# Row scaling in the sparse-attention and forgetting heads: from GpSimd to VectorE

## What is computed

```
logits = einsum(q, k) * scale + decay          # forgetting heads
p = softmax(where(causal, logits, NEG_INF))
o = p @ v

e = where(mask, exp(z - max(z)), 0)            # sparse attention, three branches
p = e / max(sum(e), 1e-30)
out = gate0 * (p_c @ v_c) + gate1 * (p_s @ v_s) + gate2 * (p_w @ v_w)
```

## Time and profile before

| | us |
|---|---|
| median of 3 runs | 2121.92 (2121.44 to 2124.77) |
| the profiled execution, its own time | 2123.0 |
| span of the profiled execution | 2121.1 |
| PE busy | 2072.8 |
| DVE busy | 1036.2 |
| ACT busy | 810.8 |
| POOL busy | 247.1 |

### The profile page before, as it was taken

The page is one execution under the profiler, slowest core; times in us unless marked ns, Lnnn a source line. Parts: engine busy times, 40 slices in busy tenths (PEclk is TensorE's granted clock), DMA queues, the critical chain, the costliest instruction groups (busy, mean ns, idle before and its releaser), DMA issues.

```text
span 2121.1 us, 25763 instructions
## 1 busy us (share of the span) xinstructions
PE 2072.8 (98%) x10471; PEld 1679.3 (79%) x10471; DVE 1036.2 (49%) x1872; ACT 810.8 (38%) x1543; POOL 247.1 (12%) x276
## 2 busy tenths in 40 slices
PE   7999999999999999999999999999999999999998
PEld 6767788888888767788888888878766788888887
DVE  6464454334436364454334436746556445433443
ACT  4355452222234355452222225344456334222222
POOL 2004410000002004310000002000267000000000
PEclk9999999999999999999999999999999999999999
DMA  5433333233322312233233332422321224323321
GB/s 157 119 65 74 97 103 99 96 95 99 94 90 76 100 50 67 81 97 100 95 94 100 95 95 57 114 62 79 87 60 31 85 90 124 100 90 100 100 95 65
DMA packets 269513, 189.42 MB, mean 89 GB/s; under 512 B 18156, under 2 KB 239524, under 8 KB 269396
## 3 DMA queue, kind: packets, MB, share of 16 engines
q1 hardware_dynamic: 264080, 174.28, 28.1%
q0 software_dynamic: 5168, 13.47, 2.6%
q10 hardware_dynamic: 148, 0.04, 0.0%
HBM read 183.53 MB, written 4.23 MB: 89 GB/s over the span
## 4 chain that ended last, share of the span: by engine, by line
PE 92%; DVE 4%; ACT 2%; POOL 1%; issue 1%; DMA 0%; DVEq 0%; ACTq 0%; POOLq 0%
PE bank L635 53%; PE bank L681 9%; PE bank L683 9%; PE bank L682 9%; PE bank L770 3%; PE bank L737 2%; PE bank L756 2%; PE bank L694 1%; PE bank L865 1%; DVE weights_hi_lo L1035 1%; PE bank L867 1%; PE bank L866 1%; ACT arena L1761 1%; PE bank L742 1%; DVE h_features L1073 1%
## 5 line engine op out<-in xcount | busy, mean ns | idle before, releaser
L635 PE MATMUL bank<-h_features,weights_hi_lo 128*128 128x512 f32 (+1 forms) x5088 | 1115.9, 380 | 5.1 <-DVE weights_hi_lo L1035 4.2
L635 PEld LDWEIGHTS bank<-h_features,weights_hi_lo 128*128 128x128 f32 x5088 | 916.8, 189 | 188.7 <-issue 6.4
L1035 DVE TENSOR_TENSOR weights_hi_lo<-weights,weights_hi_lo 128x1024 fp32r<-128x1024 f32 (+2 forms) x337 | 396.5, 1181 | 491.8 <-ACT weights_hi_lo L1702 491.1
L1702 ACT ACTIVATE weights_hi_lo<-weights 128x1024 fp32r<-128x1024 f32 (+2 forms) x337 | 337.8, 1007 | 276.3 <-PE bank L683 250.8
L681 PE MATMUL bank<-weights_hi_lo,hidden 128*128 128x512 f32 x528 | 205.8, 390 | 0.0
L683 PE MATMUL bank<-weights_hi_lo,hidden 128*128 128x512 f32 x528 | 205.4, 389 | 0.0
L682 PE MATMUL bank<-weights_hi_lo,hidden 128*128 128x512 f32 x528 | 205.4, 389 | 0.0
L1818 ACT ACTIVATE arena<-arena 128x512 f32<-128x512 f32 x66 | 41.7, 632 | 269.7 <-DVE arena L1194 269.7
L2173 POOL TENSOR_SCALAR arena<-arena,row_stats 128x256 f32<-128x256 f32 (+5 forms) x140 | 127.6, 924 | 139.6 <-DVE row_stats L1118 63.7
L1194 DVE TENSOR_TENSOR arena<-bank,arena 128x512 f32<-128x512 f32 x66 | 69.5, 1053 | 118.4 <-PE bank L635 110.9
L1821 ACT ACTIVATE hidden<-arena 128x512 fp32r<-128x512 f32 x66 | 41.7, 632 | 218.4 <-DVE arena L1200 218.4
(11 more groups left out here) (354 smaller groups left out, 2122.2 us busy)
## 6 DMA issues: line engine op xcount, KB each, us to landing
weights<-in_w_in_dram SPq DMA_DIRECT2D x78, 512.0 KB, 3.9
weights<-in_w_gate_dram SPq DMA_DIRECT2D x66, 512.0 KB, 3.8
weights<-in_w_up_dram SPq DMA_DIRECT2D x66, 512.0 KB, 3.9
weights<-in_w_down_dram SPq DMA_DIRECT2D x60, 512.0 KB, 3.6
weights<-in_w_out_dram SPq DMA_DIRECT2D x24, 512.0 KB, 3.6
bias_rows<-decay_scratch POOLq DMA_DIRECT2D x16, 256.0 KB, 4.6
weights<-in_w_in_dram SPq DMA_DIRECT2D x13, 256.0 KB, 3.2
weights<-in_w_down_dram SPq DMA_DIRECT2D x12, 256.0 KB, 2.6
```

Source lines behind the costliest of these rows:

```text
L635: last = e.matmul(out_ap, l, r, start=(j == 0), stop=(j == len(pairs) - 1))
L1035: e.tensor_tensor(pair_view(i, 1), raw_view(i), pair_view(i, 0).bitcast(F32), ALU.subtract).then_inc(done, tick(("split", i)))
L1702: e.activation(pair_view(i, 0), raw_view(i), ACT.Copy).then_inc(done, tick(("hi", i)))
```

## The change

The two multiplications of a step leave POOL's `attend` and enter DVE's, as the same `tensor_scalar` on the same rows with the same per-row factor. They stand in iteration i for step i-1, behind the copies of step i-3 and ahead of `behind(i)`, of the differential mix and of the low half of a value group. DVE first waits for its own reciprocal of that step; PE's transposes wait for DVE's count instead of POOL's. POOL keeps the loads of bias rows, which no longer stand behind a multiplication.

```
-                            pe.wait_ge(pool.done, pool[*u.name, "scaled", j])
+                            pe.wait_ge(dve.done, dve[*u.name, "scaled", j])
...
+                        if 1 <= i <= n and steps[i - 1].kind != "diff":
+                            u, st = steps[i - 1], STATS[(i - 1) % 16]
+                            dve.wait_ge(done, dve[*u.name, "norm"])
+                            for j in range(2):
+                                e.tensor_scalar(row(i - 1, j)[:, 0:u.w], row(i - 1, j)[:, 0:u.w], st[:, 6 + j:7 + j], None, ALU.mult
+                                                ).then_inc(done, tick((*u.name, "scaled", j)))
                         behind(i)
...
-                            u, st = steps[i - 1], STATS[(i - 1) % 16]
-                            if u.kind != "diff":
-                                pool.wait_ge(dve.done, dve[*u.name, "norm"])
-                                for j in range(2):
-                                    row = rows[(2 * (i - 1) + j) % 8][:, 0:u.w]
-                                    e.tensor_scalar(row, row, st[:, 6 + j:7 + j], None, ALU.mult).then_inc(done, tick((*u.name, "scaled", j)))
+                            u = steps[i - 1]
```

## The result

The changed kernel takes **2128.87 us** (median of 7 runs, 2128.51 to 2130.68) against 2122.33 us (2119.92 to 2124.77) for the kernel before, run beside it: ratio 1.0032, 95% interval 1.0022 to 1.0042, slower by 6.5 us. The forecast was 2122.8 us, "no change", with a range that ended at 2128.5 us. So the prediction was wrong: the kernel is slower by more than the 0.2% that can be told from no change, and its time lies just outside the range.

The account below looks back on a forecast made before the run. PE, busy 98% of the span, was taken as the bound. Terms 1.1 + 0.5 + 0.3 + 0.2 - 1.2 = +0.9 us, added to the median, gave 2122.8 us, "no change"; range 2119.5 to 2128.5 us.

Parts of the forecast that it names:

- Wide steps behind a branch tile: M, iterations 19 to 23 and 43 to 47: old wait for POOL and new wait swap, +0.1 us each, +0.2 us.
- M, iterations 4 to 7: Start of M: four narrow multiplications of steps 2 and 3 ahead of `first_product`, 0.7 us less a 0.2 us gap, +0.5 us.
- Forgetting steps: L0 and L1, iteration 30: multiplication of step 29 delays a value group's low half, 2 x 0.54 = +1.1 us.
- Narrow steps where POOL was waited for: Three places in M: waits for POOL go, returning 0.7, 0.3 and 0.2 us, together -1.2 us.
- Iteration 31: M: PE already waits 0.23 us for a maximum; one pair (step 27) is put ahead of it, +0.3 us.
- Wide steps behind a gate tile: M: 0.68 us of multiplications disappears in DVE's 1.00 us wait for PE and following pairs fit; no cost.
- Prices: DVE multiplication: 0.486 us record for 512 columns; 25 us more DVE work in M, less 3 us relief on two-column operations.
- The first: Rival: DVE becomes the bound in M between the fills, 2128 to 2135 us, typically 2129; chance 0.18.
- its weaker form: DVE as M's bound between the fills for a few sets only; included in that rival's chance of 0.18.
- The second rival: Faster: waits for POOL vanish and DVE's relief pays for the rest, -3 to -4.5 us, 2118.5 us; chance 0.12.
- Rivals three and four: DVE multiplies at one element a cycle, 2130 us, chance 0.02; bias-row loads come late, 2125 us, chance below 0.01.
- Eleven walks: Eleven stretches in M, each followed through the engines' waits and held good to some 0.3 us.

Follow-up runs that it names:

- pool_ahead: Changed kernel with the multiplications of M's steps 0, 1, 16, 17, 40, 41 left on POOL; 2124.53 us, ratio 1.0017 to the kernel before.
- act_first: Changed kernel with ACT copying the weight slab before its exponentials in iterations 19 and 43 of M; 2124.98 us, ratio 1.0004 to the kernel before.
- early: Changed kernel with DVE multiplying ahead of the weight split and copies, layers included; 2125.71 us, ratio 1.0017 to the kernel before.
- pool_ahead_again: The kernel of pool_ahead unaltered, repeated for a second profiled execution; stretch 19 to 23 took 12.51 us, first score to tile 11 27.84 us.
- hybrid: Changed kernel with forgetting heads and M's steps 0-3, 16, 17, 26, 27, 32-37, 40, 41 left on POOL; 2122.98 us, ratio 0.9996 to the kernel before.
- combined: Changed kernel with act_first's edit, DVE multiplying only M's steps 4-25, 28-31 and 35, POOL the rest; 2119.07 us, ratio 0.9986 to the kernel before.
- delay_b: Kernel before, POOL multiplying, with idle DVE operations ahead of M's maxima, 4 in iteration 19, 6 in 43; stretches 19 to 23 +1.98, 43 to 47 +3.89 us.

## Why the prediction was wrong, point by point

**Wide steps behind a branch tile, +0.1 us each: the step that failed.** My walk through iterations 19 to 23 began at DVE's copy at 1563.18 and held that start fixed. I wrote that the multiplications delay what is queued behind them, "the next step's maxima" and "ACT's exponentials and copies", but never carried the delay through ACT's slab copy into DVE's own split. Two pairs earlier than the walk's first row, the maxima of step 19 were late by 0.8 us, and the walk should have begun there. Measured: +2.64 and +1.32 us instead of +0.1 each. `pool_ahead` and `act_first` show the link at both ends.

**No term for the clock.** Even with the right chain I would have added idleness only. The added idleness at tile 19 is 0.44 us (beside a slower PE; `early`, at the full clock, has 0.78 us more than before); the price was 2.64 us. The profile before had the sign of it: its granted clock in M is 0.99, not 1.00.

**M, iterations 4 to 7, +0.5 us: right for what it counted, with as much left out.** The same omission: the multiplications of steps 0 and 1 delay the maxima and so the three slab copies. DVE's first copy behind the three splits begins 8.34 us after the first score instead of 7.56, and 7.65 us after it with these two steps left on POOL (`pool_ahead_again`). Where the low clock lasts through the fill, the stretch takes 24.34 us with steps 0 to 3 on POOL (`hybrid`), 25.00 us with 0 and 1 there (`pool_ahead`) and 25.61 to 25.74 us with none: the multiplications of steps 2 and 3, which I had counted, cost 0.66 us, those of steps 0 and 1 another 0.6 to 0.7, and 0.3 us comes back from 7 to 11, which leaves the 1.0 us found above. The +2.67 us of the first profile has the second fall of the clock on top.

**Forgetting steps, +1.1 us: right.** The gap of iteration 30 went from 0.48 us to 0.95 us in L0, from 0.9 to 1.9 us in both layers. No other wait of PE in the layers grew.

**Narrow steps where POOL was waited for, -1.2 us: one of three.** 23 to 27 gave -0.65 us where I had -0.7. The other two were to leave 0.3 and 0.2 us; 11 to 19 gave 0.08, and 35 to 43 lost 0.73, so this term was about 1.2 us too good. PE waits there 0.64 us for ACT's L1782 and 0.63 us for DVE's multiplication in place of 0.71 us for POOL. With steps 32 to 37 left on POOL (`hybrid`) the stretch took 16.62 us, with only step 35 on DVE (`combined`) 15.87 us, less than before's 16.38. So the pairs around step 35 cost, and its own one gains; which of them cost was not taken apart.

**Iteration 31, +0.3 us:** +0.41. **Wide steps behind a gate tile, nothing:** tile 7 to 11 -0.31 us in the second execution (13.07 against 13.38; in the first the lower clock lay in it), tile 31 to 35 -0.23, and 47 on 0, right to some 0.3 us.

**Prices.** 512 columns took 0.48 to 0.50 us, as forecast; L1112's longest time fell from 0.48 to 0.27 us, where I had none above 0.2, while its median of 0.17 us stayed:

```profile
L1138 DVE TENSOR_SCALAR junk<-junk,row_stats x8: 479/481/502, 185.8 to 873.4; 128x512 f32<-128x512 f32 x8
```
```profile
L1112 DVE TENSOR_SCALAR row_stats<-row_stats x48: 151/165/273, 1511.8 to 1645.7; 128x2 f32<-128x2 f32 x48
```

DVE's busy time in M grew by 19 us, against 25 less 3.

The Trainium skill's table (page VectorE: DVE Perf Modes, section on the TRN2 errata), from which the prediction estimated 0.33 us for 512 columns, is well under the 0.48 us of these rows. A remark under that table says that its row comes out too short for a single operation and gives a fixed term of about 150 cycles; that makes an estimate of 0.42 us, nearer but still short.

**The rivals.** The first gave 2129 us for "DVE becomes the bound in M", and the time is 2128.9; but its mechanism isn't what happened. DVE is busy 109.45 of 148.62 us, 74%, and PE waits for a maximum (L1104) once, for 0.6 us, where the rival wanted it in every wide set. `act_first` has the same DVE work with M at 142.69 us. What holds of it is at most its weaker form, a few sets only, for which I gave no price; that 2129 us came out is chance. The second rival (faster) needed the waits for POOL to turn into gain; 2.1 us of them went and 4.2 us of waits for DVE came. Rivals three and four didn't occur: the price of 512 columns is the fast one, and no wait names the bias rows.

**The range.** Eleven walks "good to some 0.3 us" each was the wrong measure of what I didn't know: the error sat in four stretches (first score to 11, 19 to 23, 35 to 43, 43 to 47), each one to three microseconds, and the range had no place for a cost that jumps.

## What to carry to other kernels

When work is put into an engine's queue, start the walk at the first row behind it and follow the delay through the *other* engines' orders too, until it comes back: here DVE, ACT's exponential, ACT's slab copy, DVE's split. An operation that waits for another engine is the worst thing to have in front of what PE needs; before moving work, look what stands behind such waits, and move the awaited copy forward instead (0.72 us at tile 19 in the kernel before, 3.4 us in the changed one). And where PE stands near its limit, price a new gap of one or two microseconds with the lower clock that may follow it, 1 to 3 us here, and not by its own length.

## What the runs showed of the hardware

- In block M the granted clock fell to 0.50 in or up to 2.5 us behind PE gaps of 1.38, 1.55, 1.65, 1.73, 1.75, 2.00, 2.47, 2.64 and 3.11 us, some of them with a second, shorter gap behind them; it stayed at 1.00 behind gaps of 0.67, 1.46 and 1.56 us, and did the one in one kernel and the other in another behind 0.96 and 0.97 us. The low stretches at tiles 19 and 43 lasted some 3 to 7 us.
- A smaller delay can cost more: 6 idle operations at tile 43 cost 3.89 us, 8 cost 3.11 us (one execution each).
- Two-column DVE operations beside a working POOL took up to 0.48 us; with POOL nearly idle (2.15 us in M) the longest of 48 took 0.27 us. For 128 columns the median was 0.42 us beside a multiplying POOL (`delay_b`) and the mean 0.27 us with POOL nearly idle (the changed kernel, M).
